# Where the context's pieces stand inside an expert pass: none between the two parts of the last product

## What is computed

```python
for gi in range(N_GROUPS):
    hid = (jax.nn.silu(jnp.einsum('td,edf->tef', t, w_gate[gi]))
           * jnp.einsum('td,edf->tef', t, w_up[gi])
           * combine[:, gi, :, None].astype(t.dtype))
    out = out + jnp.einsum('tef,efd->td', hid, w_down[gi])
```

```python
for l in range(DEPTH_2):
    hx = rmsnorm(x, g_pre[l]) * (1 + scale[:, None]) + shift[:, None]
    hc = rmsnorm(ctx, g_pre[l]) * (1 + scale_c) + shift_c
    if l % 2 == 0:
        yx, yc = mlstm_pool_mixer(hx, hc, ab_w_in[j], ..., ab_w_out[j], not last)
    else:
        yx, yc = window_attention_mixer(hx, hc, c_w_in[j], c_sink[j], c_w_out[j], not last)
    x = x + gate[:, None] * rmsnorm(yx, g_post[l])
    if not last:
        ctx = ctx + gate_c * rmsnorm(yc, g_post[l])
```

## Time and profile before

| | |
|---|---|
| time, three runs | 1762.47, 1764.61, 1775.44 us; median 1764.61 |
| the profiled execution | 1760.53 us, its span 1758.7 us |
| mean granted TensorE clock | 0.93 |
| busy | PE 1568.1, PEld 1068.4, DVE 488.3, ACT 341.5, POOL 4.1 us |
| the experts' stage on TensorE | 543.6 to 1139.3 us, and its end up to 1177.6 |
| moved by DMA | 397.57 MB, 226 GB/s over the span |

### The profile page before, as it was taken

How to read it: one execution, slowest core, us unless ns; L and a number is a source line. 1 busy time by engine, 2 the same in 40 slices (tenths; PEclk the granted TensorE clock), 3 DMA queues, 4 the chain that set the end, 5 groups by cost and what they waited for, 6 DMA issues and landing times.

```text
span 1758.7 us, 21938 instructions
## 1 busy us (share of the span) xinstructions
PE 1568.1 (89%) x9261; PEld 1068.4 (61%) x9261; DVE 488.3 (28%) x1222; ACT 341.5 (19%) x706; POOL 4.1 (0%) x8
## 2 busy tenths in 40 slices
PE   6999979899789789988998998958889999989797
PEld 3655779778675333634375645447666676767466
DVE  2200163542224321223114000035252231010681
ACT  2301240221112112011200001032212222121371
POOL 0000000000000000000000000000000000000000
PEclk8999986899879889999999999967899999989999
DMA  9988520122229898999999999922222323423000
GB/s 380 408 355 363 218 97 1 48 99 96 93 97 421 354 399 368 402 369 420 420 400 416 406 404 422 370 88 84 96 95 97 143 96 130 157 77 122 4 1 25
DMA packets 54303, 397.57 MB, mean 226 GB/s; under 512 B 6359, under 2 KB 13688, under 8 KB 16440
## 3 DMA queue, kind: packets, MB, share of 16 engines
q1 hardware_dynamic: 40384, 341.85, 48.3%
q10 hardware_dynamic: 13240, 52.16, 7.5%
q0 software_dynamic: 576, 2.10, 0.3%
HBM read 389.80 MB, written 6.29 MB: 225 GB/s over the span
## 4 chain that ended last, share of the span: by engine, by line
PE 75%; DMA 9%; DVE 7%; ACT 4%; issue 2%; PEld 1%; SPq 1%; ACTq 0%; PEldq 0%; DVEq 0%
PE bank L680 15%; PE bank L1416 11%; PE bank L1431 8%; PE bank L2343 6%; DMA work<-in_moe_w_up 6%; PE bank L2360 4%; PE bank L1531 3%; PE bank L1536 3%; PE bank L525 3%; PE bank L2329 2%; PE bank L711 2%; PE bank L1140 2%; PE bank L1128 2%; PE bank L869 1%; DMA work<-in_ab_pool_w 1%
## 5 line engine op out<-in xcount | busy, mean ns | idle before, releaser
L680 PE MATMUL bank<-H,ring 128*128 128x256 f32 (+1 forms) x928 | 242.4, 420 | 6.1 <-ACT work L1057 4.0
L680 PEld LDWEIGHTS bank<-H,ring 128*128 128x128 f32 x928 | 176.3, 192 | 64.9 <-issue 41.4
L2343 PE MATMUL bank<-ring,work 128*32 128x512 f32 (+1 forms) x768 | 139.5, 640 | 22.2 <-DMA work<-in_moe_w_up 11.7
L1416 PE MATMUL bank<-H,work 128*128 128x256 f32 x512 | 116.4, 386 | 0.3 <-issue 0.3
L1416 PE MATMUL bank<-H,ring 128*128 128x256 f32 x512 | 112.9, 381 | 0.0
L1416 PEld LDWEIGHTS bank<-H,work 128*128 128x128 f32 x512 | 97.6, 193 | 19.5 <-issue 6.4
L1416 PEld LDWEIGHTS bank<-H,ring 128*128 128x128 f32 x512 | 98.1, 192 | 13.7
L2343 PEld LDWEIGHTS bank<-ring,work 128*32 128x32 f32 (+1 forms) x768 | 36.7, 124 | 112.1 <-issue 85.0
L1431 PE MATMUL bank<-work,H 128*128 128x512 f32 x192 | 85.2, 596 | 0.0
L1431 PE MATMUL bank<-ring,H 128*128 128x512 f32 x192 | 83.0, 592 | 0.0
L2360 PE MATMUL bank<-ring,work 128*32 128x512 f32 (+1 forms) x384 | 66.8, 610 | 3.8 <-issue 2.2
(11 more groups left out here) (405 smaller groups left out, 1998.8 us busy)
## 6 DMA issues: line engine op xcount, KB each, us to landing
ring<-in_moe_w_gate SPq DMA_DIRECT2D x48, 1024.0 KB, 11.5
ring<-in_moe_w_up SPq DMA_DIRECT2D x48, 1024.0 KB, 9.5
ring<-in_moe_w_down SPq DMA_DIRECT2D x48, 1024.0 KB, 11.8
work<-in_ab_w_in ACTq DMA_DIRECT2D x28, 1024.0 KB, 10.2
ring<-in_ab_w_in SPq DMA_DIRECT2D x14, 2048.0 KB, 7.5
work<-in_ada_w SPq DMA_DIRECT2D x12, 2048.0 KB, 15.7
ring<-in_w_in SPq DMA_DIRECT2D x12, 2048.0 KB, 9.7
work<-in_w_mod SPq DMA_DIRECT2D x12, 2048.0 KB, 8.8
```

Source lines behind the costliest of these rows:

```text
L680: mm = nc.tensor.matmul(bank[i % NB][:, 0:n], weight(c, k, j * P, (j + 1) * P), rhs(k), start=(k == 0), stop=(k == kt - 1))
L1416: mm = nc.tensor.matmul(b[:, j * T:(j + 1) * T], w_k(m, n, k, at, at + P), H[:, k, m.s], start=(k == 0), stop=(k == DT - 1), skip_group_ch ...
L2343: mm = nc.tensor.matmul(bank[b][rows, :], gath[:, k, rows], half_slot[(load_at[n + half] + e) % NHALF][:, (k % 4) * 512:(k % 4 + 1) * 512] ...
```

## The change

Two tables are changed, of pieces for each place of a four and of a two:

```diff
-        FILL_FOUR, FILL_TWO = (2, 2, 2, 2, 2, 2, 2, 1, 1), (0, 0, 0, 1, 0, 1, 0, 0, 0)
+        FILL_FOUR, FILL_TWO = (2, 2, 2, 2, 3, 0, 2, 2, 2), (0, 0, 0, 1, 1, 0, 0, 0, 0)
```

## The result

The changed kernel takes 1779.7 us (median of 4 runs, 1779.0 to 1786.4) beside 1763.5 us for the kernel before (4 runs, 1758.3 to 1775.4): a ratio of 1.0100, 95% interval 1.0069 to 1.0131. Run again, with more runs of both, it is 1.0096 (1.0083 to 1.0110), or +17.0 us. So it is slower, by 9 to 10 in a thousand, which lies at the edge of what I had called no change. I had forecast +4.7 us. The sign is the forecast's, the size is more than three times as large.

The account below looks back on a forecast made before the run. It took TensorE to pace the first three four-expert passes and weight DMA the last three. Terms gave +16.8 us to the last product's end and -12.1 behind it, +4.7 in all: 1769.3 us, range 1753 to 1784.

Parts of the forecast that it names:

- my own account: Whole kernel: the summed terms hold, about +5 us, between -3 and +12; chance 0.55.
- rival 3: DMA starves after the last product, loads come late in passes 3 to 5, slow steps follow; +19 us, 1783; chance 0.18.
- pass 1: Second four-expert pass: gains two full context pieces (7.1 us), gives one cheap, 4.5 us wait stays; +6.6 us.
- pass 2: Third four-expert pass: gives two full pieces (-7.1), gains three cheap (+5.3), 2.4 us wait goes; -4.2 us.
- pass 3: Fourth four-expert pass: six full pieces behind the last product where four cheap and one or two full stood; +10.9 us.
- pass 4: Fifth four-expert pass: gains pool pieces (+18.2) and piece 89 (+3.6), gives four full (-14.2), 1.6 more wait; +9.2 us.
- pass 5: Last four-expert pass: gives pool pieces and piece 89 (-21.5), gains six full (+21.3), 2 us wait allowed; +1.8 us.
- passes 6 to 9: Two-expert passes: copy waits hidden (-2.2), pass 8's weight wait gone (-3.6), norm halves in pass 9 (-2.9); -8.7 us.
- end: Behind the last product: row scaling comes after 21 us instead of 33.1, set by row store and gathers; -12.1 us.
- The pool pieces: In pass 4: transfers issued early and covered by TensorE work, then VectorE makes four means in a row; 18.2 us.
- Rival 4: Whole kernel: nothing changes, the end gives back exactly what the passes take; 1765 us; chance 0.10.
- Rival 2: Expert stage: slots freed sooner, so waits for expert weights shrink by a further 20 us; 1749 us; chance 0.17.

Follow-up runs that it names:

- after_again: The changed kernel run again unaltered for a second trace: 1780.2 us, ratio 1.0096 to the kernel before.
- two_only: Kernel before with only the new filler table for the two-expert passes, four-expert passes as before: 1760.4 us, ratio 0.9981.
- count_17: Kernel before with only the extra context piece per four-expert pass, 17 instead of 16, old places kept: 1773.4 us, ratio 1.0059.
- late_93: Changed kernel with one context piece of pass 5 moved one step later: 1783.2 us, ratio 1.0112 to the kernel before.
- place_16: Kernel before with only the new places around the last product (3, 0, 2) in four-expert passes, still 16 pieces: 1773.1 us, ratio 1.0059.
- half_after: Changed kernel loading only half of the expert weights' bytes: 1731.4 us, ratio 0.9842 to the kernel before with all bytes.
- half_count_17: Kernel before with only the extra piece per four-expert pass, loading half the expert weights' bytes: 1738.9 us, ratio 0.9880 to the kernel before with all bytes.

## Why the prediction was right and wrong

By the bound that I set, 1% or 17.6 us, the outcome is the likeliest one, and the time lies in the range. That is partly luck: +17.0 us is just inside the bound, outside the -3 to +12 that I gave my own account, and nearer to the +19 of rival 3. The sum was 12 us too low. The changes in us, step by step, of the two profiled executions of the changed kernel (each against the one before):

| | forecast | after | after_again |
|---|---|---|---|
| pass 0 | +1.2 | +2.6 | +0.3 |
| pass 1 | +6.6 | +9.5 | +8.7 |
| pass 2 | -4.2 | -4.1 | -5.3 |
| pass 3 | +10.9 | +11.0 | +12.7 |
| pass 4 | +9.2 | +13.3 | +11.7 |
| pass 5 | +1.8 | +7.1 | +8.2 |
| passes 6 to 9 | -8.7 | -8.9 | -9.2 |
| end | -12.1 | -10.7 | -10.6 |
| sum | +4.7 | +19.8 | +16.5 |

**Right.** Passes 0, 2 and 3 within about the scatter of the two executions. In pass 2 it is for the reason given: the wait of 2.4 us is down to 0.3. Pass 3's +10.9 rests on uneven prices: pass 3 gains four full pieces (14.2 us) and gives pass 2 three cheap ones, which are put at 5.3 us in pass 2 and, by the difference, at 3.3 in pass 3; piece 21 is gained at 1.2 us and given at 0.5, so that the sum counts 2.7 us for work that only changes its pass. The twos: no wait of 0.7 us in front of the last product, no context loads beside them; passes 6 to 8 changed by -4.8 and -5.2 us for -5.8, since 1.45 and 0.78 us of wait for weights stayed in pass 8. two_only alone gains 2.9 us and not 5.8: its pass 8 still waits 4.0 us for weights, and in count_17 that wait is gone, so the two terms belong to two parts of the change, as the prediction had them. Pass 9 with the norm ahead of the product: -4.1 for -2.9. The pool pieces: 18.8 us from 929.4 to 948.2 for the 18.2 worked out. The end: the scaling waits for the gathered rows (11.12 us), 22.4 us behind the last product for 21.

**Pass 5, the pass that failed most.** "I allow 2 us of wait" was 6.0 us (3.62 for context weights, 2.4 of L1531 for VectorE), and 1.7 us for the piece that ran slowly behind the first. The first is the DMA's, as late_93 and the kernels with half the bytes show: pieces that load their own weights had come into a pass without gaps between the loads. I had the price for it in hand, 2.5 us for each MB of context weights, and did not apply it to the place where these loads had moved. The second is the context's own chain, of which I had only looked at the pool pieces.

**Passes 1 and 4.** "The wait of 4.5 us stays" in pass 1: instead there are three, 2.60, 1.43 and 1.35 us, and two of 0.72 us of L1495 for VectorE more. The three together are hardly longer, but the steps behind all of them take 5.2 to 5.3 us instead of 3.57; before, one step was slow there, 6.3 us behind the 4.5 us of wait. In pass 4 the wait of the up step is 2.9 us where I had 0.6 and 1.6 more, and TensorE's granted clock in the pass is 0.94 instead of 1.00. All in all I had counted +1.2 us of idle time in the fours (-2.4, +1.6, +2.0); it is +10.7, of which the lines that wait for VectorE or the pool transfer have 6.6 (-7.1 for the transfer, +13.7 for VectorE), the context's weights 3.3 and the expert weights 0.8. The busy time, +28.7, I had some 4 us lower. The sum had no term for the granted clock, which by the estimate above costs 8.5 us more in the fours of the first execution and 7.5 in those of the second (25.5); only rival 3 had one, of 5 us. This was the largest term left out. The sum's busy time was off by less than that because of the 2.7 us of uneven prices and of smaller differences in what the pieces took.

**The end.** 1.4 us less came back than forecast: the first row gather starts 12.8 us behind the last product instead of 10.2, since the store before it took 11.0 us to land instead of 8.5. Two loads of 2 MB for the next stage had been queued at 1159.2 and 1159.6 us, and the second landed at 1176.3, 6 us after the store was issued; before, both had landed by 1139.9, ahead of the store at 1140.2. Whether this is the reason was not tried.

**The rivals.** The last product's end at 1169 us is beyond the 1165 at which I said rival 3, the starved DMA, is right. Half of it is. place_16 shows its mechanism alone: 39.5 us of waits for weights for 25.8, in front of gate steps, as rival 3 had it, though rival 3 put it into passes 3 to 5 and it is in passes 1, 3 and 5. In the whole change these waits are hidden in the total, 27.0 us for 25.8: the seventeenth piece alone takes the waits down to 19.7 (count_17), and beside it the whole change has 7.3 more, 3.1 of them in the twos. The lower DMA share of passes 3 to 5 is fewer bytes per us because of longer passes, not more bytes or lost loads. The slow steps behind waits, rival 3's other term, are there too. Rival 4, nothing, is out by the interval. Rival 2, that the waits vanish, is out: they did not shrink in any kernel with all the bytes in which the last product's steps stand side by side. The one unknown cost that I had bounded, up to +12 us for holes in the DMA, was not the largest: the context's waits for VectorE (L1484, L1495, L1531), 6 us more, and the lower clock, 8.5 us, had no bound in the sum at all.

What stays open: whether the 9.9 us of the placement divide in the times as they do in the one profile of it, some 6 us of the DMA and 2 of VectorE (with half the bytes the intervals are too wide to say), and why TensorE was granted more clock in half_after than in half_count_17.

## What to carry to other kernels

Filler work has a price at both ends: ahead of a tail that another chain bounds, only as much is worth moving as the tail still waits for it (here pieces worth 17 us moved and 10 came back; three pieces late in the twos, where the scaling did not yet wait for the gathers, gave the lowest median, though not one that can be told from moving none). Two steps put side by side give their buffers back side by side, and the loads that follow them become one block: look at when slots come free, not only at how many. Read a longer busy time together with the granted clock before it is called work: here 8.5 of 28.7 us were the clock. Before a wait on a shared DMA is filled or moved, see whether the stretch behind it is paced by the same DMA: then the wait comes back under another name, 3.62 us as 3.09, or a pass later.

## What was not expected of the hardware

A short wait can cost more than its length. Kernel after, pass 1:

```profile
643.04 5.31 PE L2343 MATMUL bank<-ring,work 128*32 128x512 f32 x32 [1.43 <-DMA ring<-in_moe_w_up]
```

The same step took 3.6 us elsewhere; behind 3.62 us in pass 5 a piece took 5.31, and behind 3.09 us in late_93 a step took 5.25, each 1.6 to 1.7 us on top of the wait. The stretch from 643.04 to 648.35 us has a granted clock of 0.68. But it doesn't follow each time, and the same place differs from one execution to the next. The changed kernel run again, the stretch of the step behind the third wait of pass 1, 1.44 us:

```profile
653.66:657.30 3.64, 3.64 (x33) 1.01 (x33) 0.07 (x1) 0.00 (x0) 0.00 (x0) 1.00 1.02 423
```

And in pass 8 of the kernel before:

```profile
1086.98 3.65 PE L2343 MATMUL bank<-work 128*64 128x512 f32 x16 [3.59 <-DMA work<-in_moe_w_up]
```

Where a step was slow, in other executions, it took up to 6.56 us (the piece of pass 5 in after_again, at a granted clock of 0.55). So the length of the last wait alone does not tell whether the step behind it is slow.

The time of a load depends on what is queued around it, for the pool's two transfers (1 MB and 512 KB) by more than a factor of two. In the changed kernel they were issued at 908.2 and 908.6 us, when no further expert load was issued for 17 us, and landed after 10.3 and 11.1 us. In the kernel before they were issued at 903.3 and 903.8, with four expert loads issued 7 us later, and took 23.3 and 24.2 us; those four loads of 1 MB took 8.3 to 18.9 us. These are readings of two traces, not an experiment.
